# Splitting the two extra weight pieces of a border without waiting for six low halves

## What is computed

```python
x = x + 0.5 * rmsnorm(swiglu(rmsnorm(x, g), w1_gate, w1_up, w1_down), g)      # first feed-forward, 2816 wide
mixed = concat(stick_breaking(...), latent_attention(...), short_conv(...)) @ w_out
x = x + rmsnorm(mixed, g)                                                     # mixer
x = x + 0.5 * rmsnorm(swiglu(rmsnorm(x, g), w2_gate, w2_up, w2_down), g)      # second feed-forward
x = x + rmsnorm(sigmoid(rmsnorm(x, g) @ w_ple_gate) * (p @ w_ple_proj), g)    # embedding gates
```

## Time and profile before

| | us |
|---|---|
| median of 3 runs (3798.39 to 3799.4) | 3799.0 |
| the profiled execution, its own time | 3805.52 |
| its span, first to last instruction | 3804.2 |
| PE busy | 3592.0 (94%) |
| POOL busy | 2409.9 (63%) |
| DVE busy | 1708.7 (45%) |
| ACT busy | 731.0 (19%) |
| mean granted TensorE clock | 0.951 of full |

### The profile page before, as it was taken

The page is one execution under the profiler, slowest core; times in us unless marked ns, Lnnn a source line. Parts: engine busy times, 40 slices in busy tenths (PEclk is TensorE's granted clock), DMA queues, the critical chain, the costliest instruction groups (busy, mean ns, idle before and its releaser), DMA issues.

```text
span 3804.2 us, 42627 instructions
## 1 busy us (share of the span) xinstructions
PE 3592.0 (94%) x15384; PEld 2777.2 (73%) x15384; DVE 1708.7 (45%) x2048; ACT 731.0 (19%) x1449; POOL 2409.9 (63%) x1113
## 2 busy tenths in 40 slices
PE   7999999999989999999999987979999978999998
PEld 6888765788877888765788875645788867767887
DVE  6440535454146440535555136685545154244531
ACT  2110134211122110133211122215111010231100
POOL 7888730588776887731488875420688766117875
PEclk9999998999999999998999998969999999879999
DMA  3223210223322223220122321100232322002232
GB/s 115 98 96 105 89 65 8 78 89 99 105 89 79 98 94 106 88 67 12 65 96 94 109 96 69 56 34 1 83 100 94 105 94 78 23 17 89 99 98 95
DMA packets 83072, 301.81 MB, mean 79 GB/s; under 512 B 9216, under 2 KB 9472, under 8 KB 82560
## 3 DMA queue, kind: packets, MB, share of 16 engines
q1 hardware_dynamic: 80928, 292.59, 22.9%
q10 hardware_dynamic: 2016, 7.51, 0.5%
HBM read 297.97 MB, written 2.10 MB: 79 GB/s over the span
## 4 chain that ended last, share of the span: by engine, by line
PE 89%; DVE 7%; issue 2%; ACT 1%; POOL 1%; DMA 0%; ACTq 0%; POOLq 0%; DVEq 0%
PE psC L510 12%; PE psC L512 12%; PE psC L511 12%; PE psA L510 7%; PE psA L511 7%; PE psA L512 7%; PE psB L510 4%; PE psB L511 4%; PE psB L512 4%; PE psD L791 4%; PE psB L766 2%; PE psA L766 2%; PE psC L778 2%; PE psC L749 1%; PE psA L703 1%
## 5 line engine op out<-in xcount | busy, mean ns | idle before, releaser
L440 POOL TENSOR_TENSOR WH<-raw,zero 128x1024 fp32r<-128x1024 f32 (+1 forms) x554 | 1043.0, 1883 | 1326.0 <-DMA raw<-in_w 1236.2
L442 POOL TENSOR_TENSOR WL<-raw,WH 128x1024 fp32r<-128x1024 f32 (+1 forms) x554 | 1369.1, 2471 | 43.4
L510 PE MATMUL psA<-HH,WH 128*128 128x512 f32 x1216 | 487.1, 401 | 22.8 <-DVE PROJ L1434 19.8
L511 PE MATMUL psA<-HH,WL 128*128 128x512 f32 x1216 | 477.2, 392 | 0.0
L512 PE MATMUL psA<-HL,WH 128*128 128x512 f32 x1216 | 476.9, 392 | 0.0
L510 PE MATMUL psC<-HIDH,WH 128*128 128x512 f32 x1056 | 416.1, 394 | 0.0
L512 PE MATMUL psC<-HIDL,WH 128*128 128x512 f32 x1056 | 414.0, 392 | 0.0
L511 PE MATMUL psC<-HIDH,WL 128*128 128x512 f32 x1056 | 409.8, 388 | 0.0
L510 PE MATMUL psC<-HH,WH 128*128 128x512 f32 x800 | 314.9, 394 | 3.8 <-DVE HL L1360 3.8
L511 PE MATMUL psC<-HH,WL 128*128 128x512 f32 x800 | 312.9, 391 | 0.0
L512 PE MATMUL psC<-HL,WH 128*128 128x512 f32 x800 | 312.8, 391 | 0.0
(11 more groups left out here) (271 smaller groups left out, 5032.6 us busy)
## 6 DMA issues: line engine op xcount, KB each, us to landing
raw<-in_w SPq DMA_DIRECT2D x554, 512.0 KB, 3.3
X<-in_x ACTq DMA_DIRECT2D x4, 512.0 KB, 8.1
NRAW<-in_mem ACTq DMA_DIRECT2D x2, 1024.0 KB, 5.5
out<-Y SPq DMA_DIRECT2D x8, 256.0 KB, 2.1
PRAW<-in_p ACTq DMA_DIRECT2D x2, 512.0 KB, 4.3
band_raw<-in_band ACTq DMA_DIRECT2D x1, 1024.0 KB, 8.2
POSI<-in_pos ACTq DMA_DIRECT2D x2, 256.0 KB, 9.7
cf<-in_cf ACTq DMA_DIRECT2D x1, 384.0 KB, 12.7
```

The costliest lines, as they stand in the source:

```text
L440: pool.tensor_tensor(WH[j][:, 0:w], raw[j][:, 0:w], zero[:, 0:1].broadcast_to([P, w]), ALU.subtract).then_inc(w_hi, 1)
L442: pool.tensor_tensor(WL[j][:, 0:w], raw[j][:, 0:w], WH[j][:, 0:w], ALU.subtract).then_inc(w_split, 1)
L510: pe.matmul(out, WH[slot][:, w], hi[:, t], start=start and t == 0, stop=False)
L511: pe.matmul(out, WL[slot][:, w], hi[:, t], start=False, stop=False)
```

## The change

The wait of POOL between the fourth and the fifth piece of a border is taken out. The count of `hl_ready` that POOL's program keeps goes on by eight per border as before, so nothing else moves. No other engine's program is touched.

```diff
         def border():
             ring(RING)
-            pool.wait_ge(hl_ready, n.full(hl_ready, 6))
-            n.full(hl_ready, 2)
+            n.full(hl_ready, KD)
             split(RING, TILES)
             split(RING + 1, TILES)
```

## The result

| | before | after |
|---|---|---|
| median, us | 3799.0 (3793.6 to 3804.2, 11 runs) | 3807.2 (3801.1 to 3815.1, 11 runs) |
| the profiled execution, its own time | 3805.52 | 3801.13 |
| its span | 3804.2 | 3799.8 |
| its mean granted TensorE clock | 0.951 | 0.950 |

The changed kernel is slower: ratio 1.0021, 95% interval 1.0012 to 1.0030, that is +8.2 us by the medians, +4.6 to +11.4 by the interval. The forecast was +6.8, 3805.8.

A forecast was written before the change was run, and what follows sets the result against it. PE, busy 94% of the span, was taken as the bound, POOL mattering only where PE stands still or can be made to. 4 x 0 + 2 x 1.8 + 2 x 1.6 = 6.8 us on 3799.0 gave 3805.8, range 3798.5 to 3811.

The forecast's parts named there:

- How the engines disturb each other: DVE instructions with both inputs in SBUF and POOL's passes exclude each other, whole instructions in turn: +0.83 us per piece split beside chunks.
- Part 1: At all eight borders the extra pieces have landed early enough, so the four new POOL passes start at once.
- rival 4: The change does nothing: extra pieces land late or DVE's delays are all absorbed; 3799, chance 0.10.
- Part 2: Four borders to the mixer and second feed-forward: low halves end 0.2 to 1.7 us later, PE waits nowhere; 0 us.
- Part 3: Two borders out of the gates: PE's second chunk starts 1.2 us later, plus 0.6 for half clock; 1.8 us each.
- Part 4: Two borders to the gates: line 1242 ends 2.1 us later, 0.5 comes back through the clock; 1.6 us each.
- rival 2: At the gates piece 9 comes too late to get between lines 1240 and 1241; 3803, chance 0.17.
- rival 3: Faster: at the gates POOL is done before the sum of squares starts, ending about 3.4 us earlier; 3794 to 3796, chance 0.07.
- Part 5: POOL's sequencer loses eight short waits, under 0.1 us in all and in idle time; 0 us.
- Sum: All eight borders: 4 x 0 + 2 x 1.8 + 2 x 1.6 = 6.8 us slower; chance 0.46.
- Rival 1: Clock stays low everywhere: +9.0 us from borders out of and to the gates, 1 or 2 elsewhere; 3808 to 3810, chance 0.20.

## Why the prediction was right, point by point

- *How the engines disturb each other.* Right: one whole instruction at a time, the waiting one next, some 0.55 us behind a pass, 0.83 us per piece beside the chunks (2 x 2.14 against the 5.11 us from 398.15 to 403.26). The low pass listed from 400.57, in the middle of a low half that ended at 401.03, took 2.74 where one alone takes 2.34. DVE got its turn between two passes: in the eight borders of the changed kernel no low half took more than 2.84 us. The low halves took 0.91 and 1.42 in turn where 0.95 and 1.38 were said.
- *Part 1, pieces landed.* Right; all eight borders start the new passes at once (idle of POOL before piece 5 0.00 us in each), so rival 4 fell.
- *Part 2, mixer and second feed-forward: 0.* Right: 31.7 on both sides, and line 1240 and 1241 ran alone in 2.28 and 1.23 us. The -2.7 us of the four borders between the two profiles came for the most part (2.4) from the long first low half at 1873, which after happened not to have. It is piece 4's pass, which both kernels have, and falls this way or that with either.
- *Part 3, out of the gates: 1.8 each.* Measured 2.2 (34.32 against 32.15 in the mean). The wait was right, 1.1 to 1.5 us against 1.2 (second chunk at +6.12, 6.12, 6.51 and 6.27 instead of +5.01 and 5.07). The clock's part was mis-sized: 0.6, where some 1.0 remains. I took the middle of 0 and 1.2 since the stall was shorter than the one at 1873; the half level was held as there (until 8.6 to 11.8 us after the first line 1226, 10.5 at 1873). No experiment separates this remainder, but the traces do: in the sixteen borders with the wait the second chunk starts at the same place, and the border's length grows with the time at half level behind the first product, from 31.1 us at 2.9 to 32.7 at 6.2, 0.48 us for each. Without the wait this time is 6.2 to 9.5 us, 8.1 in the mean. Take the stall off it, go by that line and add the stall, and the four borders come out within 0.12 us of what they measured: on average 1.2 of stall and 0.9 of clock.
- *Part 4, to the gates: 2.1, of which 0.5 comes back.* Measured 2.07 at line 578 and 1.63 to the next border, so 0.44 came back. That this is so near to 0.5 is luck: 0.5 was the middle between two bounds, as the 0.6 of part 3 was, which did not fit. Piece 9 was before line 1241 in all six borders without the wait (the last step took 2.71 us in each), so rival 2 fell; the holding of piece 7 is rival 3's case made by hand, and it is faster, but by 5.5 us a border rather than the 3.4 named there. The 3.4 had been taken from the mixer, where line 1242 runs alone before and after (0.69 us); at the gates it too meets a pass before (2.27).
- *Part 5, the instruction itself: 0.* Right. At the start of the program the wait was already met, and there piece 5's high pass began 2.63 us after piece 4's low pass with it (24.32 and 21.69 before) and without it (25.09 and 22.46 after). The under 0.1 us for eight of them agrees with that.
- *Sum.* 2 x 2.2 + 2 x 1.6 = 7.6 us from the borders, 8.2 (4.6 to 11.4) from the times, 6.8 forecast. Rival 1's 9.0 is inside the interval of the times too; the 1 or 2 us that it adds for half clock elsewhere were an estimate that no run shows: between the borders the feed-forwards took 337.6 us in every profile, and the mixers 293.5 to 299.8 in no order of kernels. The borders lie between the two, in part 3 nearer to rival 1 (2.2 between its 2.4 and my 1.8), in part 4 at my 1.6 and not at its 2.1. The highest chance, 0.64, had gone to a result within 7.6 us of no change; 8.2 is just beyond, so the size came as forecast and that class did not. Rival 2's own terms give 3.4 (2 x 1.8 - 2 x 0.1) and not the 3.6 to 4 written there.

## What to carry to other kernels

Work of GpSimd that seems free because it fills idle time had a price here on VectorE's instructions that read two operands from SBUF (a low half took 2.45 us instead of 0.75); put it where the engine that waits for VectorE has a lead (31.7 us a border with the wait and without), and not beside the first chunk of a border where it has none yet (34.3 against 32.2) or a reduction that everything waits for (33.1 against 31.0). To find such a place read the two timelines side by side and look for instructions that end a fixed time behind the other engine's (here 0.55 us). A piece of work moved ahead of a wait is won only as far as nothing behind the wait was hidden by it (here 4.4 of 5.4 us with the whole of piece 5, nothing with half of it and piece 6 held). When single executions differ by more than the effect, compare profiles stretch by stretch from a fixed point, since two spans alone would here have given the wrong sign.

## What was not expected of the hardware

In 11 of the 44 borders to the mixer and the second feed-forward the first low half met the pass of piece 4 and took 2.7 to 2.9 us, and the border was 2.4 us longer, in whatever kernel; which borders these were changed from kernel to kernel, also where their programs did not differ. The stretch of the mixer between its borders took between 293.5 and 299.8 us. The time at half level in it was 30.7 us where it took 294.1 and 47.8 where it took 299.8. With 3792.9 to 3810.4 us for the kernel before in 31 runs, most of the scatter of one execution may well be of these two kinds; that was not tried.
